# Splitting the first megabyte of loads of a fused two-block fp32 kernel, and giving VectorE one weight remainder

## The reference

```
def rmsnorm(x, g):
    xf = x.astype(jnp.float32)
    y = xf * lax.rsqrt(jnp.mean(xf * xf, axis=-1, keepdims=True) + EPS)
    return (y * g.astype(jnp.float32)).astype(x.dtype)

def swiglu_ffn(x, w_gate, w_up, w_down):
    return (jax.nn.silu(x @ w_gate) * (x @ w_up)) @ w_down

def first_block(x, ...):
    x = x + 0.5 * swiglu_ffn(rmsnorm(x, ffn1_norm[l]), ffn1_w_gate[l], ffn1_w_up[l], ffn1_w_down[l])
    x = x + hybrid_mixer(rmsnorm(x, mix_norm[l]), w_in[l], ...)
    x = x + 0.5 * swiglu_ffn(rmsnorm(x, ffn2_norm[l]), ...)
    return rmsnorm(x, final_norm)
...
def reference(x, ...):
    x = first_block(x, ...)
    return second_block(x, ...)
```

## Time and profile before

| | us |
|---|---|
| median of 3 runs | 1629.65 |
| the profiled execution | 1630.36 |
| its span (first to last instruction) | 1627.9 |
| PE busy in the span | 1615.7 (99%) |
| DVE / ACT / POOL busy | 715.7 / 641.5 / 646.6 |
| PE's first product on real data starts at | 7.50 |

### The profile page before, as it was taken

One profiled execution on the slowest core, in us unless ns is written; L12 is line 12 of the kernel. 1 busy time (PEld: TensorE's weight loads), 2 busy tenths in 40 slices (PEclk: granted clock), 3 DMA queues, 4 the chain that ended last, 5 costly groups with the idle time before them and its releaser, 6 DMA issues.

```text
span 1627.9 us, 21967 instructions
## 1 busy us (share of the span) xinstructions
PE 1615.7 (99%) x7781; PEld 1328.6 (82%) x7781; DVE 715.7 (44%) x1147; ACT 641.5 (39%) x977; POOL 646.6 (40%) x287
## 2 busy tenths in 40 slices
PE   9999999999999999999999999999999999999998
PEld 7888888887887778888888888878888888888886
DVE  4333330205635865333332033677679641653222
ACT  6232322223525863332322133574554532444433
POOL 4444444443432024444444444443323224444444
PEclk9999999999999999999999999999999999999999
DMA  5322222225222002232323233222211212332322
GB/s 185 100 94 98 96 95 99 93 100 181 79 88 69 2 27 91 91 103 90 103 90 103 90 103 103 91 91 70 74 64 64 68 62 101 119 104 91 103 91 103
DMA packets 41954, 149.27 MB, mean 92 GB/s; under 512 B 4784, under 2 KB 4912, under 8 KB 41648
## 3 DMA queue, kind: packets, MB, share of 16 engines
q1 hardware_dynamic: 40112, 142.37, 26.0%
q10 hardware_dynamic: 1792, 6.21, 1.1%
HBM read 145.41 MB, written 2.10 MB: 91 GB/s over the span
## 4 chain that ended last, share of the span: by engine, by line
issue 47%; PE 38%; POOL 13%; ACT 1%; POOLq 1%; DVE 1%; DMA 0%; SPq 0%; DVEq 0%; ACTq 0%
POOL w_lo L506 13%; PE ps L569 8%; PE ps L571 8%; PE ps L570 8%; PE ps L698 2%; PE ps L699 2%; PE ps L697 2%; PE ps L850 1%; PE ps L863 1%; PE ps L875 1%; POOLq L514 0%; DMA w_raw<-in_units 0%; PE ps L914 0%; PE ps L883 0%; PE ps L779 0%
## 5 line engine op out<-in xcount | busy, mean ns | idle before, releaser
L506 POOL TENSOR_TENSOR w_lo<-w_raw,w_hi 128x1024 fp32r<-128x1024 f32 x260 | 631.3, 2428 | 915.4 <-ACT w_hi L1245 908.3
L1245 ACT ACTIVATE w_hi<-w_raw 128x1024 fp32r<-128x1024 f32 x259 | 275.0, 1062 | 854.3 <-PE ps L571 625.7
L569 PE MATMUL ps<-h_hi,w_hi 128*128 128x512 f32 x1032 | 403.6, 391 | 0.1
L571 PE MATMUL ps<-h_hi,w_lo 128*128 128x512 f32 x1032 | 401.7, 389 | 0.0
L570 PE MATMUL ps<-h_lo,w_hi 128*128 128x512 f32 x1032 | 401.5, 389 | 0.0
L569 PEld LDWEIGHTS ps<-h_hi,w_hi 128*128 128x128 f32 x1032 | 193.8, 188 | 42.4 <-issue 1.7
L571 PEld LDWEIGHTS ps<-h_hi,w_lo 128*128 128x128 f32 x1032 | 193.7, 188 | 40.4
L570 PEld LDWEIGHTS ps<-h_lo,w_hi 128*128 128x128 f32 x1032 | 193.8, 188 | 39.7
L569 PE MATMUL ps<-n_hi,w_hi 128*128 128x512 f32 x512 | 203.9, 398 | 1.0 <-POOL w_lo L506 1.0
L571 PE MATMUL ps<-n_hi,w_lo 128*128 128x512 f32 x512 | 199.6, 390 | 0.0
L570 PE MATMUL ps<-n_lo,w_hi 128*128 128x512 f32 x512 | 199.4, 389 | 0.0
(11 more groups left out here) (351 smaller groups left out, 1828.7 us busy)
## 6 DMA issues: line engine op xcount, KB each, us to landing
w_raw<-in_units SPq DMA_DIRECT2D x262, 512.0 KB, 3.3
x<-in_x SPq DMA_DIRECT2D x4, 512.0 KB, 7.2
w<-in_w ACTq DMA_DIRECT2D x1, 2048.0 KB, 7.7
out<-scr SPq DMA_DIRECT2D x8, 256.0 KB, 2.1
scr<-proj ACTq DMA_DIRECT2D x8, 128.0 KB, 2.4
inv_count<-in_inv_count ACTq DMA_DIRECT2D x1, 1024.0 KB, 4.8
const<-in_const SPq DMA_DIRECT2D x1, 772.0 KB, 5.3
cbias<-in_cbias ACTq DMA_DIRECT2D x1, 512.0 KB, 9.7
```

The source lines that it names most:

```text
L506: nc.gpsimd.tensor_tensor(w_lo[:, slot, :], w_raw[:, slot, :], w_hi[:, slot, :].bitcast(F32), ALU.subtract).then_inc(w_lo_done, 1)
L569: nc.tensor.matmul(ps[:, bank, :], whi, hi[:, k, :], start=(n == 0), stop=False)
L571: mm = nc.tensor.matmul(ps[:, bank, :], wlo, hi[:, k, :], start=False, stop=(n == DC - 1))
L1245: nc.scalar.activation(w_hi[:, slot, :], w_raw[:, slot, :], ACT.Copy).then_inc(w_hi_done, 1)
```

## The change

Four edits, all in the opening:

1. SP issues the first megabyte as four transfers of 256 KB in place of two of 512 KB: stream tile 0, the first half of unit 0 (columns 0 to 511, its blocks 0 to 3), stream tile 1, the second half of unit 0. Semaphores of their own (`x_first`, `half_in`) tell of the first two.
2. ACT makes the high part of unit 0 in two halves: the first between `h_hi` of tiles 0 and 1, the second after them. PE's first four products wait for the first half alone (`first_hi`).
3. The low part of unit 1 goes from POOL to DVE, behind `h_lo` of tiles 0 and 1. POOL waits for it before it goes on to unit 2, and DVE waits for POOL's low part of unit 0 before it starts.
4. `WARM` goes from 3 to 2.

```diff
-WARM = 3
+WARM = 2
@@ SP
-            stream(0)
-            weights(0)
+            for c in range(2):
+                sp.dma_start(x[:, c, :], dram["x"][c * P:(c + 1) * P, :]).then_inc(x_first if c == 0 else x_in[0], 16)
+                sp.dma_start(w_raw[:, 0, c * T:(c + 1) * T], dram["units"][0][:, c * T:(c + 1) * T]
+                             ).then_inc(half_in if c == 0 else raw_full[0], 16)
             weights(1)
             stream(2)
@@ POOL
+            pool.wait_ge(first_hi, 1)
             tail(0, 0)
-            tail(1, 1)
+            pool.wait_ge(w_lo_done, 2)
             pool.wait_ge(w_hi_done, 3)
@@ PE, first_pair
-                for u in range(2):
-                    pe.wait_ge(w_hi_done, u + 1)
-                    for k in range(2):
-                        high(u, k)
-                        rest(u, k)
+                pe.wait_ge(first_hi, 1)
+                for k in range(2):
+                    high(0, k)
+                    rest(0, k)
+                pe.wait_ge(w_hi_done, 1)
+                pe.wait_ge(w_hi_done, 2)
+                for k in range(2):
+                    high(1, k)
+                    rest(1, k)
                 high(0, 2)
                 high(1, 2)
@@ ACT, in raw_head and squares, tile 0 only
-                        act.wait_ge(x_in[c // 2], 16)
+                        act.wait_ge(x_in[c // 2] if c else x_first, 16)
@@ ACT, the opening
             for c in range(DC):
-                if c == 2:
-                    for u in range(2):
-                        first_head(u)
+                if c == 1:
+                    act.wait_ge(half_in, 16)
+                    nc.scalar.activation(w_hi[:, 0, 0:T], w_raw[:, 0, 0:T], ACT.Copy).then_inc(first_hi, 1)
+                elif c == 2:
+                    act.wait_ge(raw_full[0], 16)
+                    nc.scalar.activation(w_hi[:, 0, T:], w_raw[:, 0, T:], ACT.Copy).then_inc(w_hi_done, 1)
+                    first_head(1)
                     act.dma_start(const[:, 0:FIRST_CONST], dram["const"][:, 0:FIRST_CONST]).then_inc(small_in, 16)
@@ DVE, the opening
             for c in range(DC):
+                if c == 2:
+                    dve.wait_ge(w_lo_done, 1)
+                    dve.wait_ge(w_hi_done, 2)
+                    nc.vector.tensor_tensor(w_lo[:, 1, :], w_raw[:, 1, :], w_hi[:, 1, :].bitcast(F32), ALU.subtract).then_inc(w_lo_done, 1)
                 raw_tail(0, c, "g_ffn1")
```

More of the change, by code:

```diff
@@ L301, in build @@
         raw_m, raw_i, raw_f = (rows_of[k][0:64] for k in (4, 6, 7))
-        warm_set = sem("warm_set")
+        warm_set, x_first, half_in, first_hi = sem("warm_set"), sem("x_first"), sem("half_in"), sem("first_hi")
         proj_done = sem("proj_done")
```

## The result

The changed kernel takes 1632.28 us (median of 22 runs, 1630.96 to 1633.71) against 1629.70 for the kernel before (22 runs, 1629.41 to 1630.09). The ratio is 1.0015, 95% interval 1.001 to 1.0021: slower by 2.6 us. I had forecast 1630.1 with a range to 1631.7. The spread has also grown, from 0.7 to 2.75 us. The profiled execution of the changed kernel took 1632.28 us, its span is 1630.0. Two profiles show less of a difference than the medians, since the profiled execution of the kernel before (1630.36) was 0.66 us above its median.

A forecast was written before the change was run, and what follows sets the result against it. The prediction took TensorE to bound the kernel, so only PE's waits in the opening count. Transfers 0.1 plus the `h_lo` 2 wait 0.35 made +0.45 us on 1629.65, so 1630.1 us; range 1629.1 to 1631.7 (8 in 10).

The forecast's parts named there:

- The frame: Whole kernel: TensorE bounds it, so a change of the opening counts only through what PE waits there.
- the earlier first product: PE's first real product, unit 0: 1.7 us sooner, counted at nothing because a wait for unit 1's high part follows.
- PE never waits for POOL's low part of unit 2: Start of unit 2: POOL's low part ended 0.47 us before PE used it, and that slack was to stay.
- the point where PE passes `high(0, 2)`: PE's start on tile 2, at 9.82 us: it decides the whole opening, as PE does not wait again before unit 2.
- `h_lo` 2: Tile 2's low part on DVE, behind the moved subtraction: PE waits 0.35 us for it, bounds 0 to 0.6.
- The transfers: Opening transfers, four for two: shorter rows of unit 0 delay PE by 0.1 us, bounds -0.5 to 0.2; extra issues hidden.
- The lag of 1.1 us between bytes and landing: Opening transfers: each lands 1.1 us after its bytes have moved; used to estimate the new landings.
- Rival D: Opening: less warm work and PE's idleness lower its clock, costing 1.5 to 3.2 us; 1631.3 to 1633.0 us, chance 0.09.
- taken alone it is worth nothing: WARM 2 in the opening: dropping the third warm product changes nothing on PE's path, 0 us.
- What becomes faster: DVE and POOL no longer slow each other on `h_lo` 3 and unit 1's low part; worth nothing, PE waited for neither.
- B: Opening transfers: four small ones land sooner, up to -0.5 us, without the `h_lo` wait; 1629.2 to 1629.6 us, chance 0.20.
- C: DVE and POOL hinder each other at unit 2, or DVE's subtraction is late or slow; 1630.3 to 1632.3 us, chance 0.11.

The follow-up runs named there:

- split_only: Kernel before with only the first megabyte cut into four transfers, unit 0's high part in one piece, three warm products: 1631.60 us, ratio 1.0011.

## Why the prediction was wrong

The frame held in part: the loss is made before unit 2, the earlier first product is worth nothing, PE never waits for POOL's low part of unit 2, the subtraction takes 1.23 us. But that the point where PE passes `high(0, 2)` decides was right only at a clock at full level and with `h_lo` 2 in time. I had also written that 0.2%, 3.3 us, is what a measurement can tell from no change; the interval here is 0.06% either way, and 2.6 us lies clear of it. What failed:

- *The transfers, +0.1, bounds -0.5 to 0.2.* Measured +0.80 on PE's path in the profile after; alone, with the engines' overlap kept out, 0.66 in the median (1630.68 against 1630.02, and `high(0, 2)` at 10.07 against 9.41), and about 2 in four runs of eleven. I priced the rows' length and hid the issues, and took it that the bytes would flow at the old rate. They did not: 302 to 305 GB/s in place of 404 to 420. Either cut alone lowers the rate between 5 and 6 us, to 266 and 322. What in the queues does it is open.
- *`h_lo` 2, +0.35, bounds 0 to 0.6.* Alone it costs 0.96, on two transfers with halves 1.66. I had POOL start at 7.1; it started at 7.93 in the changed kernel (6.89 in its second profile), since unit 0 was whole only at 7.15 where I had 6.4. The lag of 1.1 us between bytes and landing was read from transfers that flowed evenly. In the changed kernel itself this wait was hidden by the slow clock; with WARM 3 it shows as 0.32.
- *Rival D, 0.09.* It happened, in both profiled executions; and 16 of the 22 runs have a mean clock of 0.997 or 0.998, where the kernel before has 0.999 or 1.000. The other six are no faster (five of them took 1632.5 to 1632.9); whether they had a slow stretch that the clock's record missed, none of them being profiled, is open. WARM alone costs 1.2 us on the kernel before, and giving the third product back to the changed kernel wins 1.2. I gave it little since a gap of 1.04 us had cost nothing before. The step that failed is the one that priced a warm product by its place on the path ("taken alone it is worth nothing"). The size, 1.6 us in the profile and 1.2 in the medians, is at or below the cheap end of my 1.5 to 3.2; that my 1.5 came near it is luck, since it rests on 3 us for which no row stood.
- *What becomes faster, counted at nothing.* Right for the order of the kernel before, but only by 0.07 us (`h_lo` 2 at 9.81, POOL at 9.88): split_only shows a 0.97 us wait once `h_lo` 2 begins behind POOL.

Of the other rivals, B did not happen (no later landing came sooner), and of C only that DVE's subtraction started late: POOL's low part of unit 2 took 2.42 us, as before.

The parts, each measured alone, do not add: 0.66, 0.96 and 1.2 are 2.8, the whole is 2.6. A late transfer, a late `h_lo` and a slow clock cover each other in part.

## What to carry to other kernels

Price a warm-up product by what it does to the level at which the next products run, not by its place on the path, and look at the distance between products rather than at the clock column alone. Cutting a transfer in two brings the first half sooner and can bring what stands behind it later; where a later transfer bounds, measure the later landings before you cut the first ones. Before an engine takes work over from another, follow what stands behind it in its own queue.

## What the runs showed of the hardware

- Cutting the first 512 KB transfer of the stream, or the one of the unit, left gaps in the DMA engines (share 0.77 and 0.82 from 5 to 6 us, against 1.00). With both cut the engines stayed busy (0.91 to 1.01), but a 2 KB packet took 97 to 124 ns in place of 84. In both cases the landing of tiles 2 and 3 was late (ACT took them up at 9.1 to 9.9 in nine profiled executions with a cut, at 8.5 to 9.0 in seven without).
- The packed trace counts a transfer's landing in sixteen semaphore updates. Those of unit 1 come between 6.60 and 7.66 us in the kernel before, between 6.80 and 8.41 in the changed one. Thirteen of the sixteen are there by 7.20 and 7.50: the last three make most of the delay.
- `h_lo` on DVE and the subtraction on POOL hold each other up by who comes first: begun 0.6 us behind POOL, `h_lo` took 2.36 in place of 0.74 us and ended 0.54 after POOL's end, while POOL kept its 2.41. Begun 0.07 us ahead of POOL, `h_lo` kept its 0.75 and POOL took 2.94.
- The clock column read 1.00 in microseconds in which products were 0.43 us apart, ahead of its first recorded rise.
